# Sums of weights written in place, two buffers for the blocks of a group, and other places for the groups in a decoder trunk's output projections

## The reference

```python
def conv_ffn(x, w_in, conv_w, conv_b, w_out):
    u = jnp.einsum('bsd,df->bsf', x, w_in)
    ...
    return jnp.einsum('bsf,fd->bsd', jax.nn.gelu(g) * val, w_out)
```

## Time and profile before

| | |
|---|---|
| median of 3 runs | 2574.27 us (2573.39 to 2575.01) |
| the profiled execution's own time | 2574.21 us |
| its span, first to last instruction | 2572.0 us |
| TensorE busy | 2547.9 us, 99% |
| VectorE busy | 1769.5 us, 69% |
| ScalarE busy | 1261.3 us, 49% |
| mean granted TensorE clock | 0.998 |
| raw chunk loads, median to landing | 3.9 us (846) |
| group block loads, median to landing | 5.9 us (64) |

### The profile page before, as it was taken

The page is one execution under the profiler, slowest core; times in us unless marked ns, Lnnn a source line. Parts: engine busy times, 40 slices in busy tenths (PEclk is TensorE's granted clock), DMA queues, the critical chain, the costliest instruction groups (busy, mean ns, idle before and its releaser), DMA issues.

```text
span 2572.0 us, 40126 instructions
## 1 busy us (share of the span) xinstructions
PE 2547.9 (99%) x14238; PEld 2221.0 (86%) x14238; DVE 1769.5 (69%) x1990; ACT 1261.3 (49%) x1409; POOL 15.9 (1%) x39
## 2 busy tenths in 40 slices
PE   9999999999999999999999999999999999999997
PEld 9999888888888888788888888888888888888886
DVE  6666667767676789875555555555767766678986
ACT  4444445555555555534444434433455555555552
POOL 0000000000000000000000000000000000000000
PEclk9999999999999999999999999999999999999999
DMA  8554574555555655655555555566555555556554
GB/s 281 176 174 162 184 245 148 197 187 197 194 196 196 209 208 202 232 176 187 180 179 179 174 187 179 181 226 190 178 197 182 201 183 198 186 199 217 205 196 147
DMA packets 142033, 496.06 MB, mean 193 GB/s; under 512 B 15616, under 2 KB 17920, under 8 KB 141952
## 3 DMA queue, kind: packets, MB, share of 16 engines
q1 hardware_dynamic: 133344, 481.22, 55.3%
q10 hardware_dynamic: 8608, 13.73, 1.7%
HBM read 492.80 MB, written 2.10 MB: 192 GB/s over the span
## 4 chain that ended last, share of the span: by engine, by line
PE 95%; DVE 2%; DMA 2%; ACT 0%; issue 0%; POOL 0%; ACTq 0%; DVEq 0%; SPq 0%; POOLq 0%
PE acc_cm L532 12%; PE acc_ab L532 11%; PE acc_ab L430 9%; PE acc_ab L433 9%; PE acc_ab L432 9%; PE acc_cm L535 6%; PE acc_ab L535 6%; PE acc_ab L447 4%; PE acc_ab L444 4%; PE acc_ab L446 4%; PE acc_cm L430 3%; PE acc_cm L433 3%; PE acc_cm L432 3%; DMA raw<-in_weights_dram 1%; PE acc_cm L697 1%; PE acc_cm L699 1%
## 5 line engine op out<-in xcount | busy, mean ns | idle before, releaser
L1164 DVE TENSOR_TENSOR w_lo<-raw,w_hi 128x1024 fp32r<-128x1024 f32 x830 | 1005.7, 1222 | 595.6 <-ACT w_hi L831 587.2
L831 ACT ACTIVATE w_hi<-raw 128x1024 fp32r<-128x1024 f32 (+1 forms) x834 | 867.7, 1054 | 661.3 <-PE acc_ab L433 233.0
L532 PE MATMUL acc_cm<-x_parts,w_hi 128*128 128x512 f32 x1408 | 480.1, 389 | 0.0
L532 PE MATMUL acc_ab<-x_parts,w_hi 128*128 128x512 f32 x1280 | 436.2, 389 | 0.0
L535 PE MATMUL acc_cm<-x_parts,w_lo 128*128 128x256 f32 x1408 | 388.6, 276 | 0.0
L535 PE MATMUL acc_ab<-x_parts,w_lo 128*128 128x256 f32 x1280 | 353.3, 276 | 0.0
L532 PEld LDWEIGHTS acc_cm<-x_parts,w_hi 128*128 128x128 f32 x1408 | 264.3, 188 | 54.8
L444 PE MATMUL acc_ab<-x_parts,w_hi 128*128 128x256 f32 x1020 | 284.8, 279 | 0.5 <-DVE x_parts L1193 0.5
L532 PEld LDWEIGHTS acc_ab<-x_parts,w_hi 128*128 128x128 f32 x1280 | 240.2, 188 | 49.8
L447 PE MATMUL acc_ab<-x_parts,w_lo 128*128 128x256 f32 x1020 | 282.2, 277 | 0.0
L446 PE MATMUL acc_ab<-x_parts,w_hi 128*128 128x256 f32 x1020 | 282.2, 277 | 0.0
(11 more groups left out here) (200 smaller groups left out, 3554.9 us busy)
## 6 DMA issues: line engine op xcount, KB each, us to landing
raw<-in_weights_dram SPq DMA_DIRECT2D x846, 512.0 KB, 3.9
pair_raw<-in_weights_dram SPq DMA_DIRECT2D x64, 512.0 KB, 5.9
ln_gain<-in_ln_g_dram ACTq DMA_DIRECT2D x16, 256.0 KB, 4.5
ln_bias<-in_ln_b_dram ACTq DMA_DIRECT2D x16, 256.0 KB, 5.8
h<-in_x_dram ACTq DMA_DIRECT2D x4, 512.0 KB, 7.7
x_t<-in_x_by_feature_dram SPq DMA_DIRECT2D x7, 256.0 KB, 7.6
raw<-in_weights_dram SPq DMA_DIRECT2D x4, 256.0 KB, 4.9
decay_sb<-in_decay_tab_dram ACTq DMA_DIRECT2D x1, 1024.0 KB, 6.8
```

What stands on the lines that cost most here:

```text
L532: pe.matmul(acc[:, f], wh[:, k, c], x_parts[:, CK * s + k].rearrange("p a n -> p (a n)"), start=s == 0 and k == 0, stop=False, skip_group_ ...
L831: return act.activation(o, i, ACT.Copy)
L1164: dve.tensor_tensor(wl, raw[:, at % RING], wh.bitcast(F32), ALU.subtract).then_inc(lo_ready, 1)
```

## The change

`pair_raw` and `pair_t` go. In their place stand two buffers, `unit_raw[0]` in region `side` and `unit_raw[1]` in region `sums`, used by the groups in turn, and each sum is written over the block that it no longer needs: T1 over B11, T3 over B12, T2 over B22, T4 over B21. So that nothing is overwritten before it is split, DVE computes the sums later: T1 behind the split of item 1, T3 ahead of that of item 2, T2 behind that of item 3, T4 behind that of item 4. SP loads in the order B11, B21, B12, B22 and waits for the group two before in place of the previous one; the first group waits for the last hidden values as before, the second for the last `low_sums`, the sixth of a layer for the assembly of the first pair (whose scratch lies in `sums`). In pairs 0 and 2 the groups stand two plain chunks earlier, in pair 3 one later, and pair 3's early chunks begin one position later. The layer norm's parameters are loaded from the end of the third group on.

```diff
-LEAD = [[12, 16, 20, 24], [4, 8, 12, 16], [12, 16, 20, 24], [2, 6, 10, 14]]
+LEAD = [[10, 14, 18, 22], [4, 8, 12, 16], [10, 14, 18, 22], [3, 7, 11, 15]]
...
-PAIR_EARLY = [None, PAIR - 10, None, PAIR - RING - 10]
+PAIR_EARLY = [None, PAIR - 10, None, PAIR - RING - 9]
...
-        pair_raw, = views(side_at, ("pair_raw", [P, 4, CK, COLS], F32))
-        pair_t = nc.alloc_sbuf_tensor_at("pair_t", [P, 4, CK, COLS], F32, offset=sums_at)
+        unit_raw = [nc.alloc_sbuf_tensor_at(f"unit_raw{i}", [P, 4, CK, COLS], F32, offset=at)
+                    for i, at in enumerate((side_at, sums_at))]
...
-                for b in (B11, B12, B21, B22):
-                    sp.dma_start(pair_raw[:, b], weights[base + at + b]).then_inc(pair_in[b], 16)
+                for b in (B11, B21, B12, B22):
+                    sp.dma_start(unit_raw[u % 2][:, b], weights[base + at + b]).then_inc(pair_in[u % 2][b], 16)
...
-                            sp.wait_ge(lo_ready, base + last + T4 + 1)
-                            load_unit(base, at)
+                    if i + 1 in unit_at:
+                        u = unit_at.index(i + 1)
+                        if u == 0:
+                            sp.wait_ge(hid_ready, FSTEPS * (layer + 1))
+                        elif u == 1:
+                            sp.wait_ge(sum_ready, UNITS * (layer + 1))
+                        else:
+                            sp.wait_ge(lo_ready, base + unit_at[u - 2] + ITEMS)
+                        if u == UNITS + 1:
+                            sp.wait_ge(pair_sum, TAPS * (2 * layer + 1))
+                        load_unit(base, u, i + 1)
...
-                            merged({UNIT_AFTER[second]: [copy_p1]}, ln_slots(stage, UNIT_AT[second][-1] + T4 + 1)),
+                            merged({UNIT_AFTER[second]: [copy_p1]}, ln_slots(stage, UNIT_AT[second][2] + ITEMS)),
...
                     if t == T1:
...
+                        dve.wait_ge(lo_ready, base + 1)
+                        dve.wait_ge(pair_in[u % 2][B12], at)
+                        o, a, b = B11, B12, B11
                     elif t == T3:
...
+                        dve.wait_ge(t_ready, 4 * n + T1 + 1)
+                        dve.wait_ge(pair_in[u % 2][B22], at)
+                        o, a, b = B12, B22, B12
                     elif t == T2:
...
+                        dve.wait_ge(lo_ready, base + 3)
+                        dve.wait_ge(t_ready, 4 * n + T3 + 1)
+                        o, a, b = B22, B22, B11
                     else:
                         dve.wait_ge(t_ready, 4 * n + T2 + 1)
...
+                        o, a, b = B21, B21, B22
-                    dve.tensor_tensor(pair_t[:, t], a, b, ALU.subtract).then_inc(t_ready, 1)
+                    dve.tensor_tensor(whole[:, o], whole[:, a], whole[:, b], ALU.subtract).then_inc(t_ready, 1)
...
-                    if m < 4:
-                        weight_sum(pair, u, m)
+                    if m == 2:
+                        weight_sum(pair, turn, u, T3)
...
+                    for t in {1: [T1], 3: [T2], 4: [T4]}.get(m, ()):
+                        weight_sum(pair, turn, u, t)
```

More of the change, by code:

```diff
@@ L345, in build_trunk @@
         second_long = sem("second_long")
-        pair_in = [sem(f"pair_in{b}") for b in range(4)]
+        pair_in = [[sem(f"pair_in{i}_{b}") for b in range(4)] for i in range(2)]
         sum_done, sum_hi_done, sum_ready = sem("sum_done"), sem("sum_hi_done"), sem("sum_ready")
@@ L387, in load_turns, with load_unit @@
                             "a p k n -> p (a k) n")).then_inc(raw_in[s], 16)
-            def load_unit(base, at):
-                for b in (B11, B12, B21, B22):
-                    sp.dma_start(pair_raw[:, b], weights[base + at + b]).then_inc(pair_in[b], 16)
+            def load_unit(base, u, at):
+                for b in (B11, B21, B12, B22):
+                    sp.dma_start(unit_raw[u % 2][:, b], weights[base + at + b]).then_inc(pair_in[u % 2][b], 16)
             def load_pairs(layer, q_out, turns):
@@ L1040, in round_item @@
                         b = (B11, B21, B22)[m]
-                        act.wait_ge(pair_in[b], 16 * (UNITS * pair + u + 1))
-                        copy(wh, pair_raw[:, b]).then_inc(hi_ready, 1)
+                        act.wait_ge(pair_in[u % 2][b], 16 * ((UNITS * pair + u) // 2 + 1))
+                        copy(wh, unit_raw[u % 2][:, b]).then_inc(hi_ready, 1)
                     else:
                         act.wait_ge(t_ready, 4 * (UNITS * pair + u) + m - 2)
-                        copy(wh, pair_t[:, m - 3]).then_inc(hi_ready, 1)
+                        b = (B11, B12, B22, B21)[m - 3]
+                        copy(wh, unit_raw[u % 2][:, b]).then_inc(hi_ready, 1)
                 def pair_stream(pair, turn, chunks, slots, behind):
@@ L1527, in low_sums, with weight_sum @@
                                       sum_parts[:, u, :, 0].bitcast(F32), ALU.subtract).then_inc(sum_ready, 1)
-                def weight_sum(pair, u, t):
-                    n, at = UNITS * pair + u, 16 * (UNITS * pair + u + 1)
+                def weight_sum(pair, turn, u, t):
+                    n, at = UNITS * pair + u, 16 * ((UNITS * pair + u) // 2 + 1)
+                    base = RING * turn + UNIT_AT[pair][u]
+                    whole = unit_raw[u % 2]
                     if t == T1:
[L1533 to L1539, removed]
+                        dve.wait_ge(lo_ready, base + 1)
+                        dve.wait_ge(pair_in[u % 2][B12], at)
+                        o, a, b = B11, B12, B11
@@ L1540, in weight_sum @@
                     elif t == T3:
-                        dve.wait_ge(pair_in[B22], at)
-                        a, b = pair_raw[:, B22], pair_raw[:, B12]
+                        dve.wait_ge(t_ready, 4 * n + T1 + 1)
+                        dve.wait_ge(pair_in[u % 2][B22], at)
+                        o, a, b = B12, B22, B12
                     elif t == T2:
-                        dve.wait_ge(t_ready, 4 * n + T1 + 1)
-                        a, b = pair_raw[:, B22], pair_t[:, T1]
+                        dve.wait_ge(lo_ready, base + 3)
@@ L1546, in weight_sum @@
+                        dve.wait_ge(t_ready, 4 * n + T3 + 1)
+                        o, a, b = B22, B22, B11
                     else:
-                        dve.wait_ge(pair_in[B21], at)
                         dve.wait_ge(t_ready, 4 * n + T2 + 1)
-                        a, b = pair_raw[:, B21], pair_t[:, T2]
-                    dve.tensor_tensor(pair_t[:, t], a, b, ALU.subtract).then_inc(t_ready, 1)
+                        o, a, b = B21, B21, B22
+                    dve.tensor_tensor(whole[:, o], whole[:, a], whole[:, b], ALU.subtract).then_inc(t_ready, 1)
@@ L1552, in split_item @@
                 def split_item(pair, turn, u, m):
                     i = UNIT_AT[pair][u] + m
-                    if m < 4:
-                        weight_sum(pair, u, m)
-                    whole = pair_raw[:, (B11, B21, B22)[m]] if m < 3 else pair_t[:, m - 3]
+                    if m == 2:
+                        weight_sum(pair, turn, u, T3)
                     wh, wl = parts(i % RING, TOKENS)
                     dve.wait_ge(hi_ready, RING * turn + i + 1)
-                    dve.tensor_tensor(wl, whole, wh.bitcast(F32), ALU.subtract).then_inc(lo_ready, 1)
+                    dve.tensor_tensor(wl, unit_raw[u % 2][:, (B11, B21, B22, B11, B12, B22, B21)[m]], wh.bitcast(F32),
+                                      ALU.subtract).then_inc(lo_ready, 1)
```

## The result

The changed kernel takes 2580.21 us (median of 9 runs, 2578.91 to 2582.44) against 2574.27 for the kernel before (9 runs): ratio 1.0021, 95% interval 1.0012 to 1.0029. It is slower by 0.21%: just above the 0.2% that the prediction called no change, with an interval that lies wholly above 1. It is 4.6 us above the forecast point of 2575.6, inside the range of 2568.5 to 2582. The profiled execution took 2579.40 us, 5.2 more than that of before.

What follows compares the result with a forecast made beforehand. TensorE, busy 2547.9 of 2572.0 us, bounds the kernel; only its waits and slow clock could change. Terms +6.4 + 3.5 - 2.9 - 4.4 - 1.2 = +1.4 on 2574.2 gave 2575.6 us, range 2568.5 to 2582 (own range 2573 to 2578).

Steps and rivals of the forecast that it cites:

- 13 steady groups: In each steady group item 5's split on VectorE ends late, so its matmuls wait 0.49 us: +6.4 us in all.
- two first groups: First groups of pairs 0 and 2, sharing VectorE with the low sums, wait 1.7 us each: +3.5 us.
- start of pair 3: Pair 3's first group one chunk later, pair 2's assembly two chunks earlier: the old waits go, -2.9 us.
- end of pair 1: Parameters loaded earlier make the raw loads there faster, so the four old waits vanish: -4.4 us.
- end of pair 3: Last product starts 30.0 us behind the last group instead of 33.9, its group 2.72 us later: -1.2 us.
- rival 2: Loads stay slow (mean landing above 5 us) at the ends of pairs 1 and 3: total 2586.6 us, chance 0.12.
- rival 3: Clock: the 6 us wait brings two dips, or parameter issues hit copy 4: 2578 to 2580 us, chance 0.14.
- Rival 1: Groups don't wait for item 5: 2569.2 us, or 2565.7 with the first groups in time too; chance 0.14.
- the 2580 which it worked out from the first: With 1.22 us between VectorE starts, not 1.135, the thirteen groups would cost 4.4 us more: 2580.

Runs made afterwards that it cites:

- t2_early: Changed kernel with T2 put behind item 2's split, ahead of item 3's: 2574.02 us, ratio 0.9999 to the kernel before.
- lead12: Changed kernel with the groups of pairs 0 and 2 back behind 12, 16, 20 and 24 plain chunks: 2578.89 us.
- pair3_at2: Changed kernel with pair 3's groups back behind 2, 6, 10 and 14 plain chunks, its early chunks one position earlier: 2577.60 us.
- pair1_at3: Changed kernel with pair 1's groups one plain chunk earlier (3, 7, 11, 15), its early chunks one position earlier: 2578.35 us.
- ln_late: Changed kernel with the layer norm's parameters loaded behind item 4 of the last group, as before the change: 2587.00 us, ratio 1.0045.
- groups_early_b: Changed kernel with T2 ahead of item 3's split, first groups behind 11, 3, 11, 2 plain chunks (pairs 0 to 3), early chunks moved along: 2568.59 us.

## Why the prediction was nearly right, and where it missed

| term | forecast | measured |
|---|---|---|
| 13 steady groups | +6.4 | 13 x 0.54 = +7.0 |
| two first groups | +3.5 | 2 x 1.8 = +3.6 |
| start of pair 3 | -2.9 | -2.9 (no wait there but the group's own) |
| end of pair 1 | -4.4 | 2.4 - 4.4 = -2.0 |
| end of pair 3 | -1.2 | 30.4 + 2.7 + 2.0 - 33.9 - 1.7 = -0.5 |
| first 20 us | 0 | +0.4 |
| sum | +1.4 | +5.6, the growth of the span |

Every term came out on the slow side or level. Together they put the time above the prediction's own narrower range (2573 to 2578) and above 2579.4, an outcome to which it gave a chance of 0.20 and for which it named rival 2 and a part of rival 3. Neither is the cause: the loads didn't stay slow, and one dip of the clock cost 0.3 us more than forecast. It was pair 1's end, and small misses in four other terms.

**Steady groups: right, and shown.** The place is item 5, and s3 and s5 start 1.37 and 5.92 us behind the group's first matmul, where 1.37 and 5.91 were forecast. The hole ahead of s3 is 0.63 us by the view, where the counting gave 0.78. t2_early moved the operation and took off 6.2 us against 6.3 expected. The price of a wait was a little low: not what the view says plus 0.27, but plus 0.31. Rival 1 had said that the groups don't wait; it fell with the first trace. The rows show 1.135 us between starts in the groups, also with source and target the same tile. The Trainium skill ("VectorE: DVE Perf Modes", The DRAIN you can't avoid) says that the next operation waits until the pipe is empty, and adds that one which is not held starts earlier. The prediction took the first statement alone; the rows, at 1.135, agree with the second. That the measured time lies at the 2580 which it worked out from the first is chance: the thirteen groups cost 0.6 us more than forecast, not 4.4.

**First groups: right.** VectorE's order came out step by step as counted, from 891.12 on in steps of 1.135. lead12 brought both groups down to the loss of a steady one.

**Start of pair 3: right.** No wait but the steady one is left. With pair 2's groups back (lead12) 1.0 us returns, with pair 3's back (pair3_at2) 0.5. No run puts both back, so how the 2.9 us divide between the two moves isn't shown.

**End of pair 1: the step that failed.** The step reads "those behind it, fed by loads 2 us faster, have 2 to 3 us of room." It counted 2.72 us for each plain chunk up to the last, and the term of -4.4 us came out at -2.0. The last four are held back and done for one half of the tokens first, 1.36 us each, as the description of the kernel's ends says for pair 3 and the code for both. At 2.72 each, chunk 54 would have been due at 9.53 + 0.50 + 10 x 2.72 = 37.2 us behind the last group's first matmul (1060.61); it was due at 1094.31 + 0.11 + 1.36 - 1060.61 = 35.2. Its split, the first of the two in the row at 1096.17, ended at 36.8 for a second reason: the loads from 1076 to 1092 took 3.1 to 5.5 us, median 4.5, where I had 3.2 for one alone and about 1 more for each one queued. Wanted by 37.2 - 0.16 = 37.0, as I believed, this split would just have been in time. So 2.1 of the 2.4 us of waits need the short spacing; whether they also need the late loads, and in what parts, is not settled. pair1_at3, with the chain started one chunk earlier, took 1.3 us off this end and left 1.1 us of waits, and it cannot tell the two apart. The remaining 0.25 us is a third thing: position 52's split ended 26.5 us behind the last group's first matmul, where I had counted 25.8 and it was wanted by 26.2.

**End of pair 3: mechanism right, size off by 0.7 us.** The last product starts at 30.4, forecast 30.0. The dip was not the 1.7 us of before but 2.0, with the wait of 6.1 in front. pair3_at2 shows that the last product follows the last group, with 1.8 of 2.72 us back in its trace. It shows too that VectorE's run is not all of it: a late load put the start at 31.3. In the changed kernel itself VectorE stands 0.47 and 0.57 us for copies at 2528.04 and 2529.84, and the last early chunk's copy waits for its load until 2541.33, as forecast.

**Loads and rival 2.** ln_late gives the slow loads that rival 2 described: 2587.0 us where it had said 2586.6. The agreement is in part luck: the last product starts 34.0 us behind the last group where the rival had 35.5, and the other terms were too low. Shown is that the parameters slowed the loads, from a median of 4.1 to 6.0 us. Without parameters the loads still took up to 5.5 us; what slows them then was not tested.

So the change holds three gains (parameters early, pair 3's start, pair 1's end) and pays with one misplaced operation in every group, and with first groups that stand too early. With that operation moved the kernel is level with the one before, and with the groups put where VectorE's run and the ends want them, 0.28% faster.

## What to carry to other kernels

When operations are reordered to write in place, write out the secondary engine's run around the point where the lookahead shrinks: an operation that filled a forced gap may leave it, and behind the gap it makes every later split late, although the engine is only two thirds busy on average. A tail that hangs on the last group starts earlier with it, but by less than the whole shift where loads are on its path too. Before giving a chunk its usual due time, look whether the last few are consumed at half the spacing.

## What the runs showed of the hardware that was not expected

How long TensorE had stood did not settle what it lost at half clock behind. Ahead of the last product, waits of 2.7 us (groups_early_b) and 3.6 us (before) were followed by a loss of 1.7 us each, waits of 6.1 to 6.2 us by 1.7 (lead12), 2.0 (here) and 2.2 (t2_early), and one of 8.1 us in ln_late by 2.7. A wait of 2.4 us at pair 3's end in the kernel before was followed by about 1.5 us, while one of 2.4 us at pair 1's end in lead12 had no dip behind it (granted clock 1.00 from 1096.70 to 1101.00).

VectorE's 1.135 us between starts held for operations that overwrite one of their own sources (2.27 us from 1042.18 to 1044.45, two starts on). Eight loads of 512 KB issued within 14.6 us, with no parameter loads issued among them, took 3.1 to 5.0 us; the fastest of four in a row took 3.2.
